# First group's gates: GpSimd takes the next even slab ahead of the combinations, and SyncE queues the combinations' stores behind both loads of a stage

## The reference

```python
u, v, z = jnp.split(h @ w_in, 3, axis=-1)          # w_in: 1024 x 6144
u = jax.nn.gelu(u)
v = layer_norm(jax.nn.gelu(v), ln_g, ln_b)
...
mixed = jnp.einsum("gts,bnsgc->bntgc", ws, vc) + b_s.T[:, :, None]   # 8 channel groups
y = u * mixed.reshape(B, S, A_WIDTH) * jax.nn.silu(z)
return y @ w_out
```

## Time and profile before

| | us |
|---|---|
| median of 3 runs | 2246.25 |
| lowest and highest run | 2244.74, 2246.75 |
| the profiled execution, its own time | 2245.24 |
| its span in the trace | 2243.5 |

### The profile page before, as it was taken

The page is one execution under the profiler, slowest core; times in us unless marked ns, Lnnn a source line. Parts: engine busy times, 40 slices in busy tenths (PEclk is TensorE's granted clock), DMA queues, the critical chain, the costliest instruction groups (busy, mean ns, idle before and its releaser), DMA issues.

```text
span 2243.5 us, 28745 instructions
## 1 busy us (share of the span) xinstructions
PE 2165.9 (97%) x10390; PEld 1808.9 (81%) x10390; DVE 1433.3 (64%) x1815; ACT 1033.1 (46%) x1898; POOL 1042.5 (46%) x636
## 2 busy tenths in 40 slices
PE   4999999999999999999999999998999999999998
PEld 4887778778888778888778888887888888888886
DVE  5966648757487863554975653966676567656753
ACT  4234446534546644445644445434444444434441
POOL 3456785945544765554675554440222232232222
PEclk9999999999999999999999999998999999999999
DMA  9788999785659795567886556988677796786644
GB/s 345 289 302 308 312 321 348 239 297 177 211 182 337 269 325 179 177 212 277 297 299 232 191 197 233 357 319 329 243 270 244 265 330 240 267 336 243 222 182 167
DMA packets 244782, 592.85 MB, mean 264 GB/s; under 512 B 20929, under 2 KB 96801, under 8 KB 244257
## 3 DMA queue, kind: packets, MB, share of 16 engines
q1 hardware_dynamic: 241680, 585.71, 72.7%
q10 hardware_dynamic: 2960, 5.30, 0.7%
HBM read 461.96 MB, written 119.54 MB: 259 GB/s over the span
## 4 chain that ended last, share of the span: by engine, by line
PE 72%; DMA 7%; DVE 6%; POOL 6%; ACT 3%; DVEq 2%; issue 2%; POOLq 1%; SPq 1%; ACTq 0%
PE ps L2246 21%; PE ps L2248 21%; PE ps L2247 21%; POOL w_lo L1097 4%; DMA w_raw<-in_a_w_in 3%; PE ps L2447 2%; DMA w_raw<-a_weights_combined 1%; PE ps L2496 1%; PE ps L2497 1%; POOL cbl L1116 1%; DVE acc L1712 1%; PE ps L2522 1%; DVE yb L1992 1%; ACT w_hi L1289 1%; DMA r<-b_input 1%
## 5 line engine op out<-in xcount | busy, mean ns | idle before, releaser
L1097 POOL TENSOR_TENSOR w_lo<-w_raw,w_hi 128x1024 fp32r<-128x1024 f32 x244 | 652.5, 2692 | 569.0 <-ACT w_hi L1289 568.7
L1289 ACT ACTIVATE w_hi<-w_raw 128x1024 fp32r<-128x1024 f32 x260 | 272.1, 1057 | 409.5 <-DMA w_raw<-in_a_w_in 370.0
L2246 PE MATMUL ps<-h,w_hi 128*128 128x512 f32 x1024 | 403.0, 394 | 8.6 <-POOL w_lo L1097 8.1
L2248 PE MATMUL ps<-h,w_lo 128*128 128x512 f32 x1024 | 398.9, 390 | 0.0
L2247 PE MATMUL ps<-h,w_hi 128*128 128x512 f32 x1024 | 398.7, 389 | 0.0
L1236 POOL TENSOR_SCALAR_AFFINE_SELECT pt<-pt 128x512 fp32r<-128x512 f32 x128 | 82.4, 644 | 392.8 <-ACT pt L1643 339.5
L2246 PEld LDWEIGHTS ps<-h,w_hi 128*128 128x128 f32 x1024 | 192.2, 188 | 53.2 <-POOL w_lo L1097 13.9
L2248 PEld LDWEIGHTS ps<-h,w_lo 128*128 128x128 f32 x1024 | 192.2, 188 | 40.7
L2247 PEld LDWEIGHTS ps<-h,w_hi 128*128 128x128 f32 x1024 | 192.4, 188 | 38.9 <-issue 0.2
L2246 PE MATMUL ps<-r,w_hi 128*128 128x512 f32 x480 | 191.9, 400 | 0.2 <-DMA r<-b_input 0.2
L2248 PE MATMUL ps<-r,w_lo 128*128 128x512 f32 x480 | 187.7, 391 | 0.0
(11 more groups left out here) (266 smaller groups left out, 4630.8 us busy)
## 6 DMA issues: line engine op xcount, KB each, us to landing
w_raw<-in_a_w_in SPq DMA_DIRECT2D x256, 256.0 KB, 3.7
w_hi<-b_weights_split SPq DMA_DIRECT2D x104, 512.0 KB, 4.3
w_lo<-b_weights_split SPq DMA_DIRECT2D x104, 512.0 KB, 5.9
w_raw<-in_a_w_in SPq DMA_DIRECT2D x52, 512.0 KB, 4.7
w_raw<-in_a_w_out SPq DMA_DIRECT2D x48, 512.0 KB, 5.2
w_hi<-v_weights_combined SPq DMA_DIRECT2D x48, 512.0 KB, 4.1
w_lo<-v_weights_combined SPq DMA_DIRECT2D x48, 512.0 KB, 5.7
w_hi<-a_weights_combined SPq DMA_DIRECT2D x32, 512.0 KB, 6.6
```

Source lines behind the costliest of these rows:

```text
L1097: g.tensor_tensor(wlo[p][:, rows_], raw[p][:, rows_], whi[p][:, rows_].bitcast(F32), ALU.subtract).then_inc(w_lo, 1)
L1289: s_.activation(whi[p][:, rows_], raw[p][:, rows_], ACT.Copy).then_inc(w_hi, 1)
L2246: t_.matmul(dst_, stat[0], mov[0], start=start, stop=False)
L2248: return t_.matmul(dst_, stat[1], mov[0], start=False, stop=stop)
```

## The change

The kernel is the same up to its order on two engines, and for i = 0 alone.

```diff
 (SP, in a_stage)
                 if q >= 1:
                     unit(first + 2 * q)
-                if q == GROUPS + 4:
+                if i == 0 and q >= 5:
+                    for c in combs_at(0, q - 1):
+                        load_comb(c)
+                    if split_at(0, q - 1) is not None:
+                        sp.wait_ge(ada_used, 6 * KT)
+                        load_split(split_at(0, q - 1))
+                if q == GROUPS + 4 or (i == 0 and q >= 4):
                     unit(first + 2 * q + 1)
                 s = split_at(i, q - 2)
                 if s is not None:
                     keep_split(s)
                 for c in combs_at(i, q - 2):
                     keep_comb(c)
-                if 1 <= q < GROUPS + 4:
+                if 1 <= q < (GROUPS + 4 if i >= 1 else 4):
                     unit(first + 2 * q + 1)
...
+                if i == 0 and q >= 4:
+                    return
                 for c in combs_at(i, q):
                     load_comb(c)
 (POOL)
                     lo(uz_unit(i, gg + 1, 0))
+                    if i == 0 and gg >= 1:
+                        split(0, 3 + gg)
+                        comb(0, 3 + gg)
                     lo(uz_unit(i, gg + 1, 1))
-                    split(i, 4 + gg)
-                    comb(i, 4 + gg)
+                    if i >= 1:
+                        split(i, 4 + gg)
```

More of the change, by code:

```diff
@@ L864, in a_stage @@
                 if s is not None:
-                    if i == 0:
-                        sp.wait_ge(ada_used, 6 * KT)
                     load_split(s)
```

## The result

| | before | changed |
|---|---|---|
| median of the runs | 2245.49 us (2242.52 to 2246.75, 4 runs) | 2267.46 us (2266.81 to 2267.97, 4 runs) |
| ratio | | 1.0095, interval 1.0083 to 1.0108 |
| profiled execution, its span | 2245.24, 2243.5 us | 2267.95, 2266.2 us |
| E(7) - E(0) | 177.76 us | 196.70 us |
| E(7) to S | 94.98 us | 98.21 us |

The changed kernel is slower by 22 us; the forecast was 2264. S is a second mark that I needed behind the gates: the first product of the next group's sums (operand "s" in PE's timeline), at 434.88 us before and at 457.06 after. The spans differ by 22.7 us: 18.9 arise between E(0) and E(7), 3.2 between E(7) and S, 0.5 behind it.

What follows compares the result with a forecast made beforehand. Bound taken: a GpSimd, VectorE and ScalarE ring, 4.9 + 16.8 + 3.8 + 2.8 = 28.3 us per gate, putting E(7) 18.9 us later; 2245.24 gives 2264.1, median 2265.1, less one: 2264.0. Range 2246 to 2272.

Steps and rivals of the forecast that it cites:

- E(7): Mixing of gate 7, the last of the first token group: forecast at 358.8 us against 339.90, +18.9 us.
- The ring: Gates of the first token group: ScalarE, GpSimd, VectorE's turns and second combination follow in sequence, 28.3 us per gate.
- ScalarE's step: Between VectorE's last combination and GpSimd's start: combination's hi, normalised v and even slab's first hi, 4.9 us per gate.
- GpSimd's run with its turns: In each gate: seven GpSimd instructions without idling, 16.8 us, plus five VectorE turns, 3.8 us.
- The signs named ahead of time: Profile after: distances about 26.5 to 31 us, mid-gate waits 3 to 5, GpSimd runs of seven, odd slab's load under 7.
- PE's clock: Rival: idle stretches in the gates lower the clock to 1.2 GHz; two gates of it give past 2280 us; chance 0.03.
- I carry any shift of E(7) to the end one for one: Behind E(7): PE's list is unchanged, so its +18.9 us reaches the end as it is.
- Even slab's load at nothing: SyncE in the gates: the even slab's load behind stores waiting for GpSimd costs nothing, with some 9 us of slack.
- the loads bound it: Rival: the even slab's load is late behind stores waiting for GpSimd; upper end of the range, no separate chance.
- Gates at PE's pace: Rival: VectorE is not held, all 12.84 us of waiting in the gates are won, 2233.4 us; chance 0.13.
- The contention: GpSimd and VectorE alternate by whole instructions: GpSimd's 2.40 us grows by 0.44 or 0.98, VectorE's also lengthen.
- a price of nothing: GpSimd and VectorE sharing SBUF interfaces would cost no time in the gates; the forecast would then be the faster rival's.

Runs made afterwards that it cites:

- run 3: Changed kernel with ScalarE rounding the combinations one gate later, behind the next even slab's hi; 2254.65 us, ratio 1.0029.
- run 4: Changed kernel with one of the two GpSimd rests of each second combination left out, the rounded part stored instead; 2256.80 us, ratio 1.0048.
- run 5: Changed kernel with VectorE's forming of the combinations left out from stage 4 on, a tiny multiplication in its place; 2257.08 us, ratio 1.0043.
- run 7: Changed kernel with matmuls of no use on PE at its waits for GpSimd in gates 2 to 7; 2270.28 us, ratio 1.0114.
- run 1: Changed kernel with GpSimd's old order put back, so SyncE's new order alone; 2253.06 us, ratio 1.0024.
- run 9: run 3 with each second combination's store behind the next even slab's load, and the last store in the output projection; 2257.82 us, ratio 1.0055.
- run 12: Changed kernel with ScalarE's roundings late, second combinations' stores behind the next even slab's load in stages 7 to 11, 1 MB less stored per gate; 2242.86 us.
- the run with fewer loads behind: Changed kernel with half of the bytes of two output projection loads left out, 1 MB less each; 2265.61 us, ratio 1.0082.

## Why the prediction was right, and where it was not

**The ring** held, in sum and in each member. ScalarE's step: 4.9 forecast, 4.9 measured. GpSimd's run with its turns: 20.6 forecast, 20.3 measured. The whole: 28.3 forecast, 27.84 to 28.05. The signs named ahead of time are there, but for the even distances, which the clock's falls made uneven: waits only in the middle of a gate (0.9 to 5.0 us each, where 3 to 5 were named), seven instructions in a run, VectorE at 2.7 to 3.4 us, the odd slab's load in 5.3 us and not mattering. Runs 3, 4 and 5 took out one member each and got its time back as far as the next bound.

**E(7)**: 358.8 forecast, 358.85 measured, by two errors that cancel. Without clock falls it is 194.3 behind E(0) (run 7), 2.4 less than forecast: 0.6 up to E(2), 0.6 in the three equal rings, 1.2 in the last two (the prediction took one us off the time for these, without working it out). The fall in the last gate gave 2.5 back. That the number is met to 0.1 us is luck; the ring is good to about 0.5 us per gate.

**"PE's clock"** stood as a rival with a chance of 0.03. The falls did come, in four gates, but the price I put on them was wrong: I let each gate pay. A ring that doesn't pass through PE absorbs what PE loses inside it; only the last gate counts, 2.5 us at E(7), and by S less than 0.6 us of them is left.

**"I carry any shift of E(7) to the end one for one"** was the step that failed: 3.2 us more are lost between E(7) and S, and run 1 loses 5.5 with no shift at all. It put what the transfers do there at nothing. PE's list there is unchanged, but not what the transfers have left over at E(7). This is the greater part of the 3.5 us between 2264.0 and 2267.46.

**"Even slab's load at nothing"** holds in the changed kernel, since GpSimd reaches the even slab later still. It fails once the ring is open: in run 3 ScalarE waits 10 us for it. The rival "the loads bound it" was thus the next bound, hidden under the ring.

**"Gates at PE's pace", 2233**: even with the ring open, that pace needs 7.5 MB in 23.56 us, which the transfers hardly do. The best order tried (run 9) won 4.9 of the 12.84 us at E(7), and run 12, with fewer bytes, 11.4; that no order could win them all isn't shown.

**The contention** by its price: the page "GPSIMD Engine Reference" of the Trainium skill, section Specifications, named it; the rows now show it again, 128x512 on VectorE 2.67 to 2.72 instead of 0.69, and the median of the combinations' lo 3.38 instead of 2.40. By a price of nothing, 2233 was the forecast.

## What to carry to other kernels

When instructions of two engines are put in a new order, follow the ring through every engine once around and add it up: work that was parallel before can become a chain, though no instruction is added. Then ask what a shifted end leaves behind: transfers put off are still to be made, and the stretch behind pays. And before reordering for PE's pace, divide the bytes of one period by the rate that the full queues show; if that is the pace already, order wins little.

## What the runs showed of the hardware

- The granted clock falls to 0.50 (1.2 GHz) in or behind waits of PE of some us and comes back by itself. In the changed kernel, after 3.15 us of waiting up to 227.90, it is 0.50 from 230 to past 236. In the run with fewer loads behind, it was at 0.50 from 228 on, before a wait of 3.19 us ended at 228.96. It doesn't follow every such wait: in the same run one of 2.35 us up to 345.23 had no fall behind it, while in the changed kernel one of 1.92 us up to 343.83 had. With matmuls in the gaps (run 7) it kept at 1.00, though waits of up to 2.44 us were left.
- GpSimd and VectorE take turns by whole instructions, and both pay (128x512 on VectorE 2.7 us instead of 0.69, 128x1024 on GpSimd 3.4 instead of 2.40), in every gate alike: the periods of four gates agree within 0.3 us.
- The transfers show a share of 1.02 to 1.04 at rates from 335 to 385 GB/s: about 338 in the gates, with stores and loads mixed, 383 to 389 in the 25 us behind E(7), in the changed kernel, the kernel before and run 1 alike.
